# Products of constants on TensorE in the pauses of stage passages

## The chip, the cores and the metric

The program runs on one core of one Trainium2 chip. A core has TensorE (PE), VectorE (DVE), ScalarE (ACT) and GpSimd (POOL), with SyncE (SP) as a queue for transfers. The metric is the device time of one execution in microseconds, the median of several runs. Everything is float32; wide products use three fp32r products (high times high, high times low, low times high) in place of one fp32 product.

## The reference

Two model blocks run one after the other on 512 tokens of width 1024. The first has dilated attention beside a gated recurrence (HGRN2) and a mixture of experts, the second two layers with adaptive modulation: layer 0 with latent attention and a gated linear recurrence over 512 latent and 256 context tokens, layer 1 with a gated delta recurrence. Cut to what matters here:

```python
def first_block(x, ...):
    h = rmsnorm(x, norm1_g)
    proj = h @ w_in                                   # 1024 x 3584
    o_attn = dilated_attention(...); o_h = hgrn2(...)
    x = x + concat(rmsnorm(o_attn), rmsnorm(o_h) * silu(gh)) @ w_out
    x = x + hier_moe(rmsnorm(x, norm2_g), ...)
    return rmsnorm(x, norm_f_g)

def second_block(x, ...):
    for layer in range(2):
        a_lat = modulate(rms_norm(h_lat, norm1_w[layer]), ...)
        o_lat, o_ctx = even_mixer(...) if layer % 2 == 0 else odd_mixer(...)
        h_lat = h_lat + ml[2] * o_lat
        h_lat = h_lat + ml[5] * sq_relu_mlp(modulate(rms_norm(h_lat, norm2_w[layer]), ...), w1, w2)
        # layer 0 does the same to the 256 context tokens
    return rms_norm(h_lat, final_norm)
```

Every `rms_norm` needs a sum over the 1024 features before any value of the normed tile is known, and the product that follows needs the normed tile.

## The kernel before

Activations lie feature-major: `E.hT` is the residual, `E.aT` the work tile, each 128 partitions x 8 feature tiles x up to 768 tokens. The program is a row of stages. Each is one `nc.Block()` that gives every engine its own instruction list, and it ends in a barrier of all engines: the next stage starts when the last of them is through. Inside a stage the order on each engine is the order in which the code is written, and semaphores join the engines. At four places (after the experts, after latent attention, after the delta recurrence and after the second MLP) a cleanup of semaphores lies behind the barrier.

Stages that the change touches, with their lines:

- `gemm` (L436) is every large projection. Its PE list takes one unit after another (a PSUM bank of 128 features x 512 or 256 tokens, 24 matmuls of L531), eight k-steps of three products. It waits for `w_low` (the weight panel's low part, L596 on ACT and L599 on DVE) and, in the first unit or units, for `x_low` at each k-step: that is the tile's low part, made just then on DVE. With `split` (the three output projections `wout1`, `wout2`, `wout3`) ACT copies a high part (L579) and DVE subtracts (L582). With `normed` (`proj1`, `proj2`, `proj3`) the tile comes from a `Normed` object.
- `Normed` (L258) finishes a norm: `sums` on PE (L271, L272) adds the last squares over partitions, `root` on ACT (L277 to L281) takes the root, `lows` on DVE (L294, L303) scales and splits. `NormedOpening` has nothing for PE to do; `NormedTwice` folds two norms into one (L353 on PE, L358 to L370 on ACT, L379 to L415 on DVE).
- With `squares`, a gemm's evacuations also make the next norm's squares: ACT L246, POOL L254.
- `mlp` (L2069 on) begins with `normed.sums`, then L2128 takes its first weight slot k by k as `x_low` arrives, and L2143 the rest.
- `hgrn` ends with group sums (L1296), ACT's root, DVE's scale (L1406), POOL's gate (L1430). `mla_units` ends with output products (L2337) and ACT's copy (L2372). `short_conv` begins with the split of its weights (ACT L3188, DVE L3241), then L3143. `delta` ends with transposes (L3588) and eight scalings on DVE (L3790). `put_out` turns and stores the result (L3887, L3888, L3897).

A float32 matmul shows as two records in the trace, an fp32r matmul as one.

Of the kernel before, what the change touches and what calls it, by code (L numbers as in the profile page):

```python
# [99 lines left out]
def setup(nc, ctx, d):  # L100
# [18 lines left out]
    E.cst = lambda name: d["cst"][:, CST_AT[name][0]:CST_AT[name][0] + CST_AT[name][1]]  # L119
    return E  # L120


# [135 lines left out]
class Normed:  # L258

    def __init__(self, E, c, name, T, scale, shift):  # L260
        sb = lambda n: c.enter_context(E.nc.sbuf_tensor(f"{name}_{n}", [P, KT, T], mybir.dt.float32r))
        self.E, self.T, self.scale, self.shift = E, T, scale, shift
        self.segs = [(0, S)] + ([(S, T)] if T > S else [])
        self.high, self.low = sb("x_high"), sb("x_low")
        self.summed, self.rooted, self.scaled, self.x_high, self.x_low = (E.sem(f"{name}_{x}") for x in (
            "summed", "rooted", "scaled", "x_high", "x_low"))
# [41 lines left out]
class NormedOpening(Normed):  # L308

    def sums(self, pe):  # L310
        pass
# [22 lines left out]

class NormedTwice(Normed):


# [98 lines left out]
def gemm(E, name, jobs, banks=8, split=None, ahead=None, normed=None, squares=None, then_fetch=None, then=None, stream=None):  # L436
# [29 lines left out]
    with ExitStack() as c:  # L466
# [56 lines left out]
        def _(pe):  # L523
            before, panel = -1, -1
            if normed:
                normed.sums(pe)

            def parts_of(u, k):
# [15 lines left out]
            for u, (j, (mms, _, _, part)) in enumerate(units):  # L544
# [28 lines left out]
                if stream:  # L573
                    stream.beside(pe, u)

        def part_of_x(eng, me):
# [610 lines left out]
def hgrn(E, qkv, H, stream, project):  # L1187
# [11 lines left out]
    with ExitStack() as c:  # L1199
# [9 lines left out]
        with nc.Block() as block:  # L1209
# [12 lines left out]
            def _(pe):  # L1222
# [102 lines left out]
                stream.fold(pe, 1)  # L1325
                sums(3)

            @block.scalar
# [740 lines left out]
def mlp(E, layer, T, W, end, ring, next_weights):  # L2069
# [15 lines left out]
    with ExitStack() as c:  # L2085
# [12 lines left out]
        with nc.Block() as block:  # L2098
# [14 lines left out]
            def _(pe):  # L2113
                normed.sums(pe)
                with pe.Fori(0, CHUNKS) as chunk:
                    for st in range(2 * ST):
# [16 lines left out]
                        for u, (n, s, a, b) in enumerate(unit):  # L2133
# [5 lines left out]
                            for k in range(KT):  # L2139
                                if u == 0 and i == 0:  # L2140
                                    pe.wait_ge(h_low, NT + HT * chunk + k + 1)
                                for p, (w, x) in enumerate(((wh, high), (wh, low), (wl, high))):
                                    last = pe.matmul(bank(st, n, s, b - a), w[:, st % 2, k, n * P:(n + 1) * P], x[:, k, a:b],  # L2143
                                                     start=(k == 0 and p == 0), stop=(k == KT - 1 and p == 2))
                            last.then_inc(full, 1)

            @block.scalar
# [136 lines left out]
def mla_units(E, qh, kh, V, project):  # L2284
# [9 lines left out]
    with ExitStack() as c:  # L2294
# [6 lines left out]
        with nc.Block() as block:  # L2301
# [5 lines left out]
            def _(pe):  # L2307
# [33 lines left out]
                for t in range(n + 5):  # L2341
                    if t < n:
                        scores(t)
                    if 3 <= t <= n + 2:
                        turns(t - 3)
                    if t >= 5 and t % 2:
                        outputs((t - 5) // 2)

            @block.scalar
# [750 lines left out]
def short_conv(E, w, q, k, vc, xh, xl, ring, own, gates, constants):  # L3100
# [12 lines left out]
    with ExitStack() as c:  # L3113
# [7 lines left out]
        with nc.Block() as block:  # L3121
# [9 lines left out]
            def _(pe):  # L3131
                def turn_keys(m, bank):
                    for i, (ch, j) in enumerate((ch, j) for ch in (m, m + 1) for j in range(2)):
                        last = pe.transpose(E.bank(bank)[:, i * P:(i + 1) * P], k[:, ch, j].rearrange("a g t -> a (g t)"), E.ident)
                    last.then_inc(turned, 1)
                for n in range(tiles):
                    pe.wait_ge(w_low, n + 1)
# [156 lines left out]
def delta(E, G, O, room, more, gate_dram, project, constants):  # L3294
# [8 lines left out]
    with ExitStack() as c:  # L3303
# [25 lines left out]
        def region(u, r):  # L3329
# [13 lines left out]
            "W", "W_out", "KG", "ke", "qd", "N0"))  # L3343
        uu, ws, vna, vnv, ds, st, sg, oo, oadd, gate_in, os_, squared, rooted, normed_p, normed_v, turned = (sem(f"delta_{n}") for n in (
            "U", "WS", "vn_act", "vn_dve", "DS", "S", "SG", "O", "O_add", "gate_in", "OS", "squared", "rooted", "normed_pool",
            "normed_dve", "turned"))

# [21 lines left out]
        with nc.Block() as block:  # L3369
# [9 lines left out]
            def _(pe):  # L3379
# [197 lines left out]
                for late in range(2):  # L3577
                    for u, (i, h) in enumerate(out_units):
# [11 lines left out]
                        if late:  # L3590
                            last.then_inc(turned, 1)

            @block.scalar
# [83 lines left out]
            def _(dve):  # L3677
# [110 lines left out]
                for u, (i, h) in enumerate(out_units):  # L3788
                    dve.wait_ge(turned, u + 1)
                    dve.scalar_tensor_tensor(out=E.aT[:, i:i + 5:4, 256 * h:256 * h + 256], in0=E.bank(u).rearrange("p (g n) -> p g n", g=2),  # L3790
                                             scalar=E.v("gdn_o_norm_2", 0), in1=gate[:, i:i + 5:4, 256 * h:256 * h + 256],
                                             op0=ALU.mult, op1=ALU.mult)

# [161 lines left out]
```

## Time and profile before

| | us |
|---|---|
| median of 3 runs (2991.27 to 2994.41) | 2993.59 |
| span of the profiled execution | 2994.6 |
| PE busy in it | 2787.2 (93%) |
| VectorE, ScalarE, GpSimd busy | 1152.1, 940.6, 403.4 |

No time of its own is given for the profiled execution beyond its span; the span lies 1.0 us above the median, so sums made on the span are carried over to the median unchanged. A busy PE is not PE at its peak: the trace also has the granted clock of TensorE, 1.00 for the full 2.4 GHz and 0.50 for 1.2 GHz, for each stretch. Where PE has been still, or has done little, that clock is found at 0.50 some microseconds on. "Idle before" in a row is what the engine waited, with the instruction that ended it.

### The profile page before, as it was taken

What the parts mean: (1) busy time and instruction counts of PE and PEld (TensorE: products, weight loads), DVE (VectorE), ACT (ScalarE), POOL (GpSimd) and SP (SyncE); (2) the same over time, 40 slices, a digit from 0 to 9 for tenths busy, and PEclk for the clock granted to TensorE, in tenths of its full rate; (3) what the DMA queues carried; (4) which work ended last, traced back from release to release, by engine and by line L of the source; (5) the groups of instructions that cost most, each with busy time, mean ns of one, the idle gap of its engine ahead of it and who ended that gap; (6) DMA issues with size and microseconds to landing.
All of it is one profiled execution on the core that took longest, in us unless ns stands there. A gap on an engine that the chain in (4) does not pass through costs nothing. (4 is left out here: it accounts for less than half of the span.)

```text
span 2994.6 us, 50282 instructions
## 1 busy us (share of the span) xinstructions
PE 2787.2 (93%) x21610; PEld 2080.0 (69%) x21610; DVE 1152.1 (38%) x1626; ACT 940.6 (31%) x1542; POOL 403.4 (13%) x332
## 2 busy tenths in 40 slices
PE   8988889999998998999999999998997788799999
PEld 6764654444444884747878888887786777678887
DVE  3225342223324317264442323234344455443333
ACT  4235331111112226145331212123373445432222
POOL 0014120000001302045100000010002555200001
PEclk9999889999999999789999999999997899999999
DMA  6547719999994111000121212120310000223331
GB/s 243 197 149 271 264 57 386 402 403 406 400 404 155 49 43 57 24 29 1 57 71 57 70 56 70 56 70 28 103 49 30 4 4 4 87 97 98 98 97 57
DMA packets 153632, 389.56 MB, mean 130 GB/s; under 512 B 9471, under 2 KB 100506, under 8 KB 140666
## 3 DMA queue, kind: packets, MB, share of 16 engines
q1 hardware_dynamic: 141226, 198.40, 19.4%
q10 hardware_dynamic: 12240, 188.75, 15.4%
q8 instruction: 129, 2.11, 0.3%
q14 instruction: 37, 0.30, 0.0%
HBM read 381.36 MB, written 5.77 MB: 129 GB/s over the span
## 5 line engine op out<-in xcount | busy, mean ns | idle before, releaser
L2143 PE MATMUL ps<-mlp_h_low,mlp_w_high 128*128 128x512 f32 (+1 forms) x768 | 272.0, 354 | 0.0
L2143 PE MATMUL ps<-mlp_h_high,mlp_w_high 128*128 128x512 f32 (+1 forms) x768 | 271.9, 354 | 0.0
L2143 PE MATMUL ps<-mlp_h_high,mlp_w_low 128*128 128x512 f32 (+1 forms) x768 | 271.6, 354 | 0.0
L1997 ACT ACTIVATE mlp_w_high<-mlp_ring 128x2048 fp32r<-128x2048 f32 x64 | 122.2, 1912 | 316.2 <-PE ps L2143 316.2
L2143 PE MATMUL ps<-mlp_x_low,mlp_w_high 128*128 128x512 f32 (+1 forms) x576 | 204.0, 354 | 0.0
L2143 PE MATMUL ps<-mlp_x_high,mlp_w_high 128*128 128x512 f32 (+1 forms) x576 | 203.9, 354 | 0.0
L2143 PE MATMUL ps<-mlp_x_high,mlp_w_low 128*128 128x512 f32 (+1 forms) x576 | 203.7, 354 | 0.0
L254 POOL TENSOR_TENSOR aT<-aT 128x512 f32<-128x512 f32 (+1 forms) x30 | 59.6, 1986 | 1030.5 <-ACT aT L246 1029.9
L2001 DVE TENSOR_TENSOR mlp_w_low<-mlp_ring,mlp_w_high 128x2048 fp32r<-128x2048 f32 x64 | 146.5, 2292 | 62.8 <-ACT mlp_w_high L1997 62.8
L2207 DVE SCALAR_TENSOR_TENSOR hT<-ps,mod,hT 128x512 f32<-128x512 f32 x96 | 63.5, 661 | 256.0 <-PE ps L2143 256.0
L2143 PEld LDWEIGHTS ps<-mlp_h_high,mlp_w_high 128*128 128x128 f32 x768 | 145.2, 189 | 20.5
L2143 PEld LDWEIGHTS ps<-mlp_h_high,mlp_w_low 128*128 128x128 f32 x768 | 145.1, 189 | 20.2
L2143 PEld LDWEIGHTS ps<-mlp_h_low,mlp_w_high 128*128 128x128 f32 x768 | 145.3, 189 | 19.9
L1863 DVE TENSOR_TENSOR hT<-hT,ps 128x512 f32<-128x512 f32 x128 | 79.3, 682 | 181.4 <-PE ps L1699 181.4
L2196 DVE TENSOR_TENSOR mlp_square<-mlp_relu 128x768 f32<-128x768 f32 (+1 forms) x64 | 52.7, 825 | 249.1 <-ACT mlp_relu L2165 248.8
L2165 ACT ACTIVATE mlp_relu<-ps 128x512 f32<-128x512 f32 x96 | 49.7, 527 | 296.1 <-PE ps L2143 218.4
L3143 PE MATMUL ps<-odd_x_high,conv_w_parts 128*128 128x512 f32 (+1 forms) x448 | 121.3, 359 | 3.1 <-DVE conv_w_parts L3241 3.1
L2143 PEld LDWEIGHTS ps<-mlp_x_high,mlp_w_high 128*128 128x128 f32 x576 | 108.9, 189 | 15.4
L2143 PEld LDWEIGHTS ps<-mlp_x_low,mlp_w_high 128*128 128x128 f32 x576 | 108.9, 189 | 15.0
L2143 PEld LDWEIGHTS ps<-mlp_x_high,mlp_w_low 128*128 128x128 f32 x576 | 108.8, 189 | 15.1
L1704 PE MATMUL ps<-e_wu,aT 128*64 128x512 f32 x512 | 116.9, 598 | 0.0
L1704 PE MATMUL ps<-e_wg,aT 128*64 128x512 f32 x512 | 116.2, 595 | 0.7 <-ACT aT L1784 0.7
(561 smaller groups left out, 6011.0 us busy)
## 6 DMA issues: line engine op xcount, KB each, us to landing
mlp_ring<-in_mlp_w_dram SPq DMA_DIRECT2D x64, 1024.0 KB, 5.3
e_wg<-in_w_gate_dram ACTq DMA_DIRECT2D x15, 4096.0 KB, 14.7
e_wu<-in_w_up_dram ACTq DMA_DIRECT2D x15, 4096.0 KB, 14.3
ring<-in_w_down_dram ACTq DMA_DIRECT2D x15, 4096.0 KB, 13.8
ring<-in_ada_w_dram SPq DMA_DIRECT2D x16, 2048.0 KB, 8.9
h_rest<-in_ada_w_dram SPq DMA_DIRECT2D x8, 2048.0 KB, 8.5
ring<-in_w_in_dram SPq DMA_DIRECT2D x6, 2048.0 KB, 11.2
proj_ring<-in_even_w_in_dram SPq DMA_DIRECT2D x8, 1024.0 KB, 5.1
```

The costliest lines, as they stand in the source:

```text
L254: pool.tensor_tensor(total, self.square_of(self.E, 0, self.T) if n == 1 else total, self.square_of(self.E, n, self.T), ALU.add)\
L1704: last = pe.matmul(E.ps[SLOTS * s:SLOTS * (s + 1), bank * BANK:(bank + 1) * BANK], xg[:, par, k, half * P + s * SLOTS:half * P + (s + 1) * ...
L1863: dve.tensor_tensor(E.hT[:, n, 0:S], E.hT[:, n, 0:S], E.bank(4 + n % 4), ALU.add).then_inc(added, 1)
L1997: act.activation(self.high[:, slot], self.ring[:, slot], ACT.Copy).then_inc(self.w_high, 1)
L2001: dve.tensor_tensor(self.low[:, slot], self.ring[:, slot], self.high[:, slot].bitcast(FP), ALU.subtract).then_inc(self.w_low, 1)
L2143: last = pe.matmul(bank(st, n, s, b - a), w[:, st % 2, k, n * P:(n + 1) * P], x[:, k, a:b], start=(k == 0 and p == 0), stop=(k == KT - 1 a ...
L2165: act.activation(r[:, n, a:b], bank(st, n, s, b - a), ACT.Relu).then_inc(relus, 1)
L2196: dve.tensor_tensor(sq[:, n, :], r[:, n, :], r[:, n, :], ALU.mult).then_inc(squares, 1)
L2207: dve.scalar_tensor_tensor(out=E.hT[:, k, a:b], in0=bank(st, n, s, b - a), scalar=E.mod[:, layer, 40 + k, s:s + 1], in1=E.hT[:, k, a:b], o ...
L3143: last = pe.matmul(E.bank(2 * (n % 3) + half, b - a), wp[:, part, n % 2, kk, :], xp[:, kk, a:b], start=(kk == 0 and i == 0), stop=(kk == K ...
```

## The change

A helper issues a number of matmuls of two constant tiles (all ones as weights, the identity as data, both float32, 128 x 128) into a PSUM bank that nobody reads before it is written again. It is called at seventeen places: behind the norm's sums (20 in `proj1`, 32 in `proj2`, 18 in `proj3` and in each MLP), at the start of the three output projections (11), of the short convolution (12), and at the ends of stages (14 in `hgrn`, 6 in latent attention, 6 at the end of each output projection, 11 at the end of each MLP, 22 in `delta`). That is 233 matmuls. Where the bank may still be read, PE first waits: at an output projection's end for the evacuation of that bank, at an MLP's end for all evacuations but the last step's, in `delta` for the first of DVE's eight scalings, which gets a new semaphore. Nothing is taken out, and no other engine gets an instruction.

```diff
+def constant_products(E, pe, bank, count):
+    for _ in range(count):
+        pe.matmul(E.bank(bank, P), E.ones, E.ident, start=True, stop=True)
...
 class Normed:
+    pause = 18
 class NormedOpening(Normed):
+    pause = 20
 class NormedTwice(Normed):
+    pause = 32
...
@@ gemm, tensor
             if normed:
                 normed.sums(pe)
+                constant_products(E, pe, 0, normed.pause)
+            elif split:
+                constant_products(E, pe, 0, 11)
...
                 if stream:
                     stream.beside(pe, u)
+            if squares:
+                who, n = freed_at[len(units) - banks]
+                pe.wait_ge(freed[who], n)
+                constant_products(E, pe, len(units) % banks, 6)
@@ hgrn, tensor
                 stream.fold(pe, 1)
                 sums(3)
+                constant_products(E, pe, 5, 14)
@@ mlp, tensor
                 normed.sums(pe)
+                constant_products(E, pe, 0, normed.pause)
                 with pe.Fori(0, CHUNKS) as chunk:
...
                             last.then_inc(full, 1)
+                pe.wait_ge(added, U * (ST * CHUNKS + ST - 1))
+                constant_products(E, pe, 0, 11)
@@ mla_units, tensor
                         outputs((t - 5) // 2)
+                constant_products(E, pe, 0, 6)
@@ short_conv, tensor
+                constant_products(E, pe, 0, 12)
                 for n in range(tiles):
@@ delta, tensor
                             last.then_inc(turned, 1)
+                pe.wait_ge(first_out, 1)
+                constant_products(E, pe, 0, 22)
@@ delta, vector
+                    if u == 0:
+                        ins.then_inc(first_out, 1)
```

PE at the end of `delta` and the start of `wout3` before (L3588 are the transposes of the output, L3369 and L522 the ends and starts of blocks):

```order
L3380 MATMUL ps<-gdn_vn,gdn_qk 64x128 x16
L3588 MATMUL ps<-base,gdn_O 128x2x64 x32
L3369 UNCONDITIONAL_BRANCH
L522 UNCONDITIONAL_BRANCH
L531 MATMUL ps<-wout_x_high,wout_w_high 128x512
L531 MATMUL ps<-wout_x_low,wout_w_high 128x512
L531 MATMUL ps<-wout_x_high,wout_w_low 128x512
```

And with the change, where the helper is L126 and all lines lie some 12 to 25 further down:

```order
L3405 MATMUL ps<-gdn_vn,gdn_qk 64x128 x16
L3613 MATMUL ps<-base,gdn_O 128x2x64 x32
L126 MATMUL ps<-base 128x128 x22
L3394 UNCONDITIONAL_BRANCH
L534 UNCONDITIONAL_BRANCH
L126 MATMUL ps<-base 128x128 x11
L546 MATMUL ps<-wout_x_high,wout_w_high 128x512
L546 MATMUL ps<-wout_x_low,wout_w_high 128x512
```

Behind the last transpose stand 22 products ahead of the block's end, and 11 more stand ahead of the first real product of the next block.

PE at the end of `wout3` and the start of the second MLP before (L271 and L272 are the norm's sums; the two ISA rows set up the loop over the MLP's chunks):

```order
L531 MATMUL ps<-wout_x_low,wout_w_high 128x512
L531 MATMUL ps<-wout_x_high,wout_w_low 128x512
L466 UNCONDITIONAL_BRANCH
L2112 UNCONDITIONAL_BRANCH
L271 MATMUL ps<-aT,base 128x512
L272 MATMUL ps<-aT,base 128x512
```

And with the change:

```order
L126 MATMUL ps<-base 128x128 x6
L478 UNCONDITIONAL_BRANCH
L2132 UNCONDITIONAL_BRANCH
L279 MATMUL ps<-aT,base 128x512
L280 MATMUL ps<-aT,base 128x512
L126 MATMUL ps<-base 128x128 x18
L2136 UNCONDITIONAL_BRANCH
```

Six products follow the projection's last one, and 18 lie between the norm's sums and the loop whose first product waits for the normed tile.

## Rows read from the trace of the kernel before

**Rows 1.** The page: span of the profiled execution, and its instructions.

```profile
span 2994.6 us, 50282 instructions
```

**Rows 2.** Windows: stretch, us, busy us (xcount) PE/PEld/DVE/ACT/POOL, PEclk, DMA share, GB/s

```profile
23.05:28.63 5.58, 5.58 (x13) 4.42 (x14) 5.58 (x10) 2.53 (x4) 0.00 (x0) 0.50 1.05 410
345.60:349.50 3.90, 3.90 (x9) 3.11 (x10) 3.90 (x7) 3.11 (x6) 0.00 (x0) 0.50 0.80 244
967.27:970.70 3.43, 3.42 (x10) 2.85 (x11) 3.43 (x7) 1.48 (x3) 1.77 (x1) 0.50 0.00 0
1429.38:1434.90 5.52, 5.52 (x13) 4.41 (x14) 5.52 (x7) 4.54 (x6) 0.00 (x0) 0.50 0.69 268
1508.60:1513.40 4.80, 4.80 (x14) 4.06 (x15) 4.80 (x10) 2.24 (x4) 0.00 (x0) 0.50 0.01 2
2049.40:2052.70 3.30, 3.30 (x7) 1.52 (x5) 2.36 (x2) 2.23 (x2) 0.00 (x0) 0.50 0.00 0
2058.03:2063.00 4.97, 4.96 (x12) 3.95 (x13) 4.97 (x10) 2.24 (x4) 0.00 (x0) 0.50 0.00 2
2117.71:2121.00 3.29, 3.29 (x8) 2.61 (x9) 1.09 (x1) 0.00 (x0) 0.00 (x0) 0.50 1.08 398
2570.25:2575.00 4.75, 4.75 (x11) 3.77 (x12) 4.75 (x8) 3.11 (x6) 0.00 (x0) 0.50 1.01 353
2623.74:2629.60 5.86, 5.86 (x14) 4.60 (x15) 5.86 (x10) 2.90 (x5) 0.00 (x0) 0.50 0.35 121
```

**Rows 3.** Windows view: the pause ahead of the first projection, same columns.

```profile
16.40:18.40 2.00, 0.00 (x0) 0.00 (x0) 0.00 (x0) 1.73 (x4) 0.51 (x1) 1.00 1.07 405
18.40:23.05 4.65, 0.00 (x0) 0.03 (x1) 4.51 (x6) 2.28 (x4) 0.00 (x0) 0.50 1.05 409
```

**Rows 4.** Windows view of line 3897 at half and full clock, line 531 at full.

```profile
2981.50:2984.50 3.00, 3.00 (x14) 3.00 (x15) 0.50 0.00 0
2984.70:2989.70 5.00, 5.00 (x47) 5.00 (x46) 1.00 0.51 208
...
352.00:382.00 30.00, 30.00 (x135) 24.82 (x133) 1.00 0.50 216
```

**Rows 5.** Waits view of PE: us in total, times, longest us.

```profile
PE ps L2128 <- DVE mlp_x_low L303: 8.9, 2, 5.2
...
PE ps L531 <- DVE odd_x_low L303: 6.4, 4, 5.2
```

**Rows 6.** Timeline: how VectorE hands parts over, and where proj2's first units end.

```profile
977.04 1.84 DVE L415 SCALAR_TENSOR_TENSOR even_x_low<-aT,mod,even_x_high 128x512 fp32r<-128x512 f32 x2 [0.51 <-POOL even_x_high L427]
...
985.84 0.39 PE L531 MATMUL ps<-even_x_high,proj_w_high 128*128 128x512 f32 x1
...
1428.29 7.03 DVE L582 TENSOR_TENSOR wout_x_low<-aT,wout_x_high 128x768 fp32r<-128x768 f32 x8
```

**Rows 7.** Timeline: what ends last in four stages, and PE's last sums in hgrn.

```profile
336.76 2.05 PE L1296 MATMUL ps<-hg_sq,base 128*128 128x512 f32 x2
...
340.97 1.26 POOL L1430 TENSOR_TENSOR aT<-aT,h_rest 128x512 f32<-128x512 f32 x1 [3.98 <-DVE aT L1406]
...
1424.36 0.38 ACT L2372 ACTIVATE aT<-ps 128x256 f32<-128x256 f32 x1 [0.76 <-PE ps L2337]
...
2560.45 5.36 DVE L3790 SCALAR_TENSOR_TENSOR aT<-ps,vcol,gdn_vt 128x512 f32<-128x512 f32 x8 [1.39 <-PE ps L3588]
...
2975.67 1.26 POOL L254 TENSOR_TENSOR aT<-aT 128x512 f32<-128x512 f32 x1 [8.15 <-ACT aT L246]
```

**Rows 8.** Timeline of ACT ahead of proj3: the root's first step waits for PE.

```profile
2052.91 0.81 ACT L279 ACTIVATE aT<-ps 128x768 f32<-128x768 f32 x1 [1.26 <-PE ps L272]
```

**Rows 9.** Timeline: start of the short convolution (ACT, PE) and of the output stage.

```profile
2115.35 2.00 ACT L3188 ACTIVATE conv_w_parts<-odd_room 128x1024 fp32r<-128x1024 f32 x2 [8.41 <-PEq L466]
...
2117.71 0.80 PE L3143 MATMUL ps<-odd_x_high,conv_w_parts 128*128 128x512 f32 x1 [3.11 <-DVE conv_w_parts L3241]
...
2978.06 0.56 PE L3887 MATMUL ps<-base,aT 128*128 128x1 f32 x2 [3.13 <-PEq L3869]
```

## What the change should do to the time

> **What bounds the kernel now.** I read the page first, then the windows view over every 25 us, then the waits of PE, then the timeline around each place that the change touches. The profiled execution spans 2994.6 us [rows 1]; the median is 2993.59, and I take the sum from the median, since nothing hints that the 1.0 us between them would change. PE is busy 93% of it, so a microsecond taken off PE's own work counts unless something else is late there. The reader is to see in [rows 2] ten stretches in which PE works without a break and yet at a granted clock of 0.50, the 1.2 GHz level. Each lies behind a pause in which PE waited for a norm or for the high and low parts of a tile. [rows 3] shows how it comes about at the first projection: for two microseconds of stillness the clock is still 1.00, then it is 0.50, and it stays there until some microseconds of dense matmuls have gone by. The change fills such pauses with matmuls that nobody needs. So three questions set the time: do they hold the clock up, what is half-clock work worth where it stands, and where do they stick out of the pause.
>
> **What one product costs.** The trace has no product of ones and identity. The nearest is L3897: float32, 128 x 128, other weights each time, two records per matmul. At full clock some 46 records lie in 5.00 us, 0.11 each, so 0.22 us a product; at half clock 14 lie in 3.00 us, so 0.43 [rows 4]. I take 0.22 where PE was at work until shortly before. The same rows say that this form counts as work for the clock: it ran at 0.50, and behind it the clock was 1.00. Calls of 6, 11, 12, 14, 18, 20, 22 and 32 are then 1.3, 2.4, 2.6, 3.1, 4.0, 4.4, 4.8 and 7.0 us.
>
> **What the full clock is worth, stage by stage.** A 512-wide fp32r product takes 5.58/13 = 0.43 us at half clock [rows 2], and at full clock 30.00 us hold 135 records with those cut by the edges, so about 0.225 [rows 4].
> - `proj1`: 13 products in 5.58 us would take 2.93, a gain of 2.6. VectorE's parts come no slower than PE takes them, and PE does not wait again behind the first.
> - `wout1`: 9 products, 3.90 against 2.03, gain 1.9. `wout3`: 11, 4.75 against 2.48, gain 2.3. MLP of layer 1: 14, 5.86 against 3.15, gain 2.7.
> - `wout2` has 768 tokens, and VectorE's eight parts take 7.03 us, to 1435.32 [rows 6], 0.88 each against 3 x 0.225 = 0.68 of PE. With full clock the first unit ends at 1435.32 + 0.68 = 1436.0. Before, 13 of 24 were done at 1434.90 [rows 2], and 11 more end at 1437.4. Gain 1.4, not the 2.8 that half of 5.52 would be.
> - `proj2`: the part that came late ends at 977.04 + 1.84 = 978.88 [rows 6], and three k-steps lie behind it. One is six 512-wide and six 256-wide products, 1.35 + 0.7 = 2.05 to 2.1 us. So the first units end at 985.0 to 985.2 in place of 985.84 [rows 6]. Gain 0.6 of the 1.7 that half of 3.43 would be.
> - MLP of layer 0: half of 4.80 is 2.4; its k-step costs VectorE about as much as PE, so I take 2.2.
> - `proj3`: of PE's four waits for `odd_x_low` only one is 5.2 us, and three share 1.2 [rows 5]. These three come later: PE had caught up with VectorE although it began at half clock. Gain 0.1.
>
> That is 2.6 + 1.9 + 2.3 + 2.7 + 1.4 + 0.6 + 2.2 + 0.1 = 13.8 us.
>
> Two more come from elsewhere. Eleven products at the end of layer 0's MLP lie beside the last evacuation, square and addition there, and keep the clock up for the sums ahead of `proj3`, which ran at 0.50 [rows 2]. ACT waited 1.26 us for them [rows 8], behind its table load: gain 1.3, and if the clock falls in between, 0. In `short_conv` the first tile's stretch of 3.29 us at half clock [rows 2] would give 1.6.
>
> **Where the products stick out.** A stage ends when its last engine is through.
> - `hgrn`: PE's sums end at 338.81 less the drain, POOL's gate at 342.23 [rows 7]. Fourteen take 3.1 us if the clock is up, 6.0 if not. It is at 0.50 there, but PE has then been at work for three microseconds and the clock should rise within a few of the products. Cost between 0 and 0.9 (all of them slow: 2.6); I take 0.3.
> - Latent attention: PE is through at about 1424.3, ACT at 1424.74 [rows 7]. Six more end at 1425.6: cost 0.9, since behind this barrier everything starts, ACT's split of the next tile too. It would be 2.2 at half clock.
> - `delta`: the first of the eight scalings ends at 2561.1, the last at 2565.81 [rows 7]; 22 products end at 2566.0 to 2566.3 with the drain: cost 0.4, at half clock up to 2.5.
> - Layer 1's MLP: PE had been idle for 3.13 us when it began L3887 at 2978.06 [rows 9], that is from 2974.93. Eleven end at 2977.3, POOL's addition ended at 2976.93 [rows 7]: cost 0.4. In return the output stage starts at full clock. Its first sixteen records are one column wide and may not hold it. I take 1.1 for the stage with the 0.4 taken off; the bounds are -0.4 (clock falls at once) and +3 (it holds all through 6.5 us that ran at half).
> - Short convolution: the block starts at 2115.35, its first real product at 2117.71 [rows 9]. Twelve end at 2118.0: cost 0.3.
> - Layer 1's MLP start: the shorter wait for `mlp_x_low` is 8.9 - 5.2 = 3.7 us [rows 5], 18 products are 4.0. Cost 0.2.
> - The other calls are covered: 20 in `proj1` by the 6.65 us of [rows 3], 32 in `proj2` and 18 in two places by DVE's scaling and ACT's root, which nothing of PE holds up; 11 ahead of each output projection by ACT's copy and DVE's two subtractions; 6 at an output projection's end by the last evacuation and ACT's square. If that cover were gone, each would cost its own 1.3 to 7.0.
>
> The added wait in `delta` queues nothing behind it but the products. DVE, ACT, POOL and the queues get no work, and their loads start as PE frees them.
>
> **The sum.** 13.8 + 1.3 + 1.6 + 1.1 - 0.3 - 0.9 - 0.4 - 0.3 - 0.2 = 15.7 us, so 2993.6 - 15.7 = 2977.9, say 2978.
>
> **Rivals.**
> 1. *Every half-clock microsecond gives back half.* The gated stretches are worth more than I grant because VectorE's lead is not as thin as I read it. The eight tile stretches of [rows 2] last 38.8 us together, half is 19.4 against my 13.8: 15.7 + 5.6 = 21.3, so 2972. Against it speak the waits of [rows 5] and the pace of L582. The Trainium skill, "TensorE: Matmul & The Clock Gate", terms table, gives the penalty of throttled time as that time times one less the clock's share, which is this 19.4; the trace agrees on the price of one product and not on what the stage gets.
> 2. *The tails are slow.* In `hgrn`, latent attention and `delta` the work ahead is thin, and the clock is down when the products begin: 2.3 + 1.3 + 2.1 more, and `wout2` starts behind it with its eleven products late, 1 more: net 9, so 2985.
> 3. *The loads become late.* In `proj1` and `wout3` the DMA share is 1.05 and 1.01 [rows 2]; if the weights there come no earlier than before, those 2.6 and 2.3 go, and `short_conv` (1.08) with 1.3: 2984. Against it: PE has no wait for a load in these stages, and each panel is split a unit ahead.
> 4. *Slower: constants do not count as work.* Then the clock falls as before, and each call costs 0.43 a product. 20 (8.6 us) stick out of their pause by 2.9, 32 (13.8) by 5, 11 ahead of output projections (4.7) by 1.6 three times, 18 (7.7) by 2.5 to 4 three times, 12 by 2.8, 22 by 4.7, 14 by 2.6, the tails of 6 and 11 by some 5: together about 36, so 3030. It decides as soon as the calls run at half clock throughout; with a rise in each it is rival 2. L3897 speaks against it.
> 5. *Nothing much.* The clock falls once more between the last product and the real work, where gaps of 0.7 to 2 us stay. Two thirds of the gain go: 2989.
>
> **How the numbers follow.** My forecast has 0.56, rival 1 0.12, rival 2 0.12, rival 3 0.08, rival 4 0.04, rival 5 0.08. A measurement of this kernel can tell about 0.2%, 6 us, from no change. Faster by more: the forecast and rivals 1 to 3, 0.88, less 0.02 for the edges: 0.86. Within: 0.10. Slower: 0.04. The range takes in rivals 1 to 3 and the unknown of the tails: 2970 to 2987.
>
> **What would show it.** In the profile after, the ten stretches should show a clock near 1.00 at the first real products, the products 0.22 us each, `proj3` and `proj2` end their first units hardly sooner, and the barrier behind latent attention and `delta` should open later by 0.9 and 0.4. I am wrong if the products show 0.43 in most places, or if the first units end no earlier although the clock is up.

## The result

The changed kernel takes 2965.93 us (median of 6 runs, 2958.55 to 2969.06) against 2990.02 us (6 runs, 2977.62 to 2994.41) of the kernel before; the ratio is 0.9922, with a 95% interval of 0.9904 to 0.994. Forecast were 2978 us, between 2970 and 2987. The direction was right, the time lies 12 us under the forecast and 4 under the end of the range. The gain read off the ratio is 23 us, between 18 and 29; 15.7 had been forecast. Of the six executions of before three are those that the forecast's 2993.59 rests on; the other three, timed later, have a median of 2984.62.

The page of the profiled execution (2956.7 us, where before had 2994.6, [rows 1]) and the row with the span and the mean granted clock:

```profile
span 2956.7 us, 51214 instructions
...
PE 2801.8 (95%) x22076; PEld 2104.2 (71%) x22076; DVE 1151.6 (39%) x1626; ACT 940.7 (32%) x1542; POOL 404.5 (14%) x332
```

```profile
core 0: 2956.7 us, clock 0.977
```

The same row of before:

```profile
core 0: 2994.6 us, clock 0.956
```

The 233 products made PE busier (2801.8 us, 2787.2 before) and the kernel shorter. Next, windows of PE of the changed kernel (stretch, us, PE busy (records), granted clock, DMA share, GB/s): the call in `proj1`, the first real products behind ten of the calls, and at last the output stage.

```profile
17.60:22.31 4.71, 4.70 (x40) 1.00 1.06 412
23.23:26.25 3.02, 3.02 (x13) 1.00 1.05 405
341.90:343.95 2.05, 2.05 (x9) 1.00 0.80 177
958.40:962.50 4.10, 4.10 (x26) 1.00 0.00 0
1414.40:1417.40 3.00, 3.00 (x11) 1.00 1.05 410
1492.23:1495.10 2.87, 2.87 (x16) 1.00 0.03 10
2029.90:2032.60 2.70, 2.70 (x9) 1.00 0.00 0
2038.30:2041.30 3.00, 2.60 (x10) 1.00 0.03 8
2098.40:2101.60 3.20, 3.20 (x16) 1.00 0.92 328
2538.40:2540.90 2.50, 2.50 (x11) 1.00 1.06 367
2589.90:2593.10 3.20, 3.20 (x15) 1.00 0.51 182
2941.60:2947.00 5.40, 5.40 (x34) 0.69 0.01 3
```

These answer [rows 2]: every stretch that ran at 0.50 there is at 1.00 here, and thirteen records of `proj1` lie in 3.02 us in place of 5.58. The first row gives the price of a product: 40 records in 4.70 us, 0.235 us a product, where 0.22 was assumed. Of these places only the output stage still has a part at the lower clock.

PE's waits (us in total, times, longest) where it now meets VectorE:

```profile
PE ps L546 <- DVE odd_x_low L311: 4.3, 7, 1.6
...
PE ps L546 <- DVE wout_x_low L601: 1.3, 3, 0.6
PE ps L2149 <- DVE mlp_x_low L311: 1.2, 1, 1.2
```

In `proj3` four waits have become seven ([rows 5]): PE is faster and waits for VectorE more often, and the first units end no sooner (61.34 us in both, in the table below). That is what the forecast put at 0.1 us.

### The profile page after: what moved, and what is told of

Read it like the earlier page. It is cut to its first block and busy times, and to the rows that moved or that the text cites. A ratio compares the mean times of both kernels' runs of the same rounds, so it can differ in the third digit from the quotient of the medians.

```text
span 2956.7 us, 51214 instructions
## 1 busy us (share of the span) xinstructions
PE 2801.8 (95%) x22076; PEld 2104.2 (71%) x22076; DVE 1151.6 (39%) x1626; ACT 940.7 (32%) x1542; POOL 404.5 (14%) x332
## 3 DMA queue, kind: packets, MB, share of 16 engines
q10 hardware_dynamic: 12240, 188.75, 15.7%
```

## Where the time went between the two traces

The two spans differ by 37.9 us, more than the medians do. I followed pairs of operations of VectorE, ScalarE and GpSimd, which are the same in both kernels, through both traces, and took the time from one to the next. 16 us of the difference lie at the calls, 22 in stages that no call touches; most of these are light stages, with short matmuls and waits between the engines. The two largest are the delta recurrence (8.3 us, taken up at the end) and the middle of latent attention with its gated recurrence (7.8 us). The windows of the second in the changed kernel, and in a second execution of the very same program (run `e5_changed_again`, below), same columns:

```profile
1197.90:1295.70 97.80, 92.26 (x454) 0.83 0.05 18
```

```profile
1201.80:1307.50 105.70, 99.16 (x462) 0.74 0.05 17
```

One program, the same instructions, 97.8 and 105.7 us, with a clock of 0.83 and 0.74. Before took 105.6, as long as the second execution of the changed kernel, so 7.8 of the 22 us can't be put down to the change: single executions differ by that much. The Trainium skill, "TensorE: Matmul & The Clock Gate", Part 1, says that the number of matmuls at the lower clock varies between runs of one kernel; the two rows agree. It also puts the penalty of the ramp at under 1% of a typical kernel's span. Here the clock's row of before, 0.956, is well above that, and the mere spread of before's executions is 24 us, 0.8%.

The Trainium skill's terms table in "TensorE: Matmul & The Clock Gate" prices throttled time at that time times one less the clock's share. The profile's mean clock already has that share in it, so by its two rows the price is 2994.6 x 0.044 less 2956.7 x 0.023, or 64 us; the spans differ by 38. As a rule for the difference of these two traces it is an upper bound; for one stage where PE waits for other engines in part of the time, run `e10_rope_too` below shows why.

## Experiments

`e1`, `e8`, `e9` and `e13` are the kernel before with the products that are named and no other; all others are the changed kernel with calls taken out, or moved where said. Each was timed in 6 to 12 executions (`e9` in one), beside 23 to 28 of before on the same chip. The ratio has its 95% interval behind it; a difference "by the medians" is the plain one. The two can make the size of an effect differ by up to 5 us, and both are given where it matters.

**The size of the effect, and a repetition.** No edit.

```diff
 (the changed kernel as it is)
```

> The changed kernel again, against more executions of before: before was 2983.6 us by the median of 28 executions in the last call, 10 us under its first three. If my sum of 15.7 us is right and the first executions of before were slow ones by chance, the ratio is 0.9947 and lies below 0.9965 and above 0.993. If the 22 us beyond the sum that the two traces show belong to the change, it is 0.9922 or less.

Measured: 2966.05 us (6 runs), ratio 0.9918 (0.989 to 0.9945). All executions of before beside the experiments of this section, 101 of them, have a median of 2985.5 us between 2974.6 and 2998.7, and 20 of them lie at or over 2991.2. The three on which the forecast's level stood were all over 2991.2. Twelve executions of the changed kernel have 2966.05. So 8 of the 12 us by which the forecast's time was off are the level, and the effect is 19.5 us by these medians. By the two ratios (0.9922 and 0.9918) it is 23 to 24. The expectation had named a ratio of 0.9947, between 0.993 and 0.9965, if 15.7 us were right, and that did not come: even the upper end of the interval, 0.9945, is below it, and the ratio itself is at the value (0.9922 or less) that stood for a gain beyond the sum. The effect is therefore larger than the forecast's, by 4 us as the medians have it and by 8 as the ratios have it.

**`proj1` alone.**

```diff
+    pause = 20   (NormedOpening; no other call, every other pause 0)
```

> The kernel before with the 20 products of proj1 and none of the other calls. The whole change gained 24 us by its median, and its trace shows 16 of them where the prediction put them and 22 us in stages that no call touches. Theory A (the rest is a matter of where the light stages come to lie in time: any shift ahead of them moves them into or out of half clock): proj1 gains 2.5 us, and the trace shows latent attention, its recurrence and delta some us shorter or longer than in the trace of before although not one of their instructions is another; the ratio is 0.9992 with up to 0.003 either way. Theory B (products at the ends of stages hold the clock up into the light work behind them): nothing but proj1 changes beyond some tenths of a us, ratio 0.9992. Theory C (luck of single executions, the same in both kernels): ratio 0.9992, and the trace differs from before's in the light stages, but the median does not.

Measured: 0.9983 (0.9968 to 0.9997), 2981.33 against 2983.57 us by the medians, 2.2 us. All three theories had 0.9992, which the interval holds, so the time decides between none of them. The trace has the first unit at 12.65 us between two evacuations around it, against 15.26 in before. The middle of latent attention took as long as in before (105.6), delta 290.2 in place of 294.0, with nothing of them edited.

**A mere delay.** Three products in the middle of `proj2`, where PE is at work at full clock without a break.

```diff
+                if isinstance(normed, NormedTwice) and u == 12:
+                    constant_products(E, pe, u % banks, 3)
```

> The kernel before with three products in the middle of proj2, where PE is at work at full clock without a break, and nothing else: a pure delay of 0.7 us of all that follows. In four of the six traces the middle of latent attention, with the gated recurrence, took 105.6 us with 54.6 at half clock, in two 97.9 with 34.1, and the two began 1 us later against the steps of the clock. Theory A (when the light stages begin decides how much of them runs at half clock): the stretch takes 97.9 us although it only starts 0.7 later, and the kernel as a whole is 2 to 7 us faster than before, by a mere delay. Rival (what the change's products do for the clock decides): the stretch takes 105.6 as before, and the kernel is 0.7 us slower.

Measured: 0.9998 (0.9984 to 1.0011). The window of the same middle of latent attention:

```profile
1207.20:1301.10 93.90, 88.68 (x466) 0.85 0.06 19
```

11.7 us shorter than in before, behind a delay alone, though the part ahead of it took 4.5 more (101.6 against 97.1). Theory A had expected a shorter stage and a kernel faster by 2 to 7 us; the second did not come. That the delay is what made the stage shorter is not shown: it is one trace, and the changed kernel gave 97.8 and 105.7 us without any edit. In sixteen traces this middle took 105.6 to 105.8 us seven times and 93.1 to 99.0 nine times, with and without the change's calls. So the stage falls into one of a few lengths in each execution, and neither the calls nor the delay is shown to choose it.

**The ends of stages, without and alone.** Taken away (`e2`), alone (`e3`), and alone with the 18 products in the MLPs (`e7`).

```diff
 e2_no_ends (each with its wait, where it has one)
-                constant_products(E, pe, 5, 14)               (hgrn)
-                constant_products(E, pe, len(units) % banks, 6)   (output projections)
-                constant_products(E, pe, 0, 11)       (end of mlp)
-                constant_products(E, pe, 0, 6)        (mla_units)
-                constant_products(E, pe, 0, 22)       (delta)
```

> The changed kernel without the products at the ends of stages (14 in hgrn, 6 in latent attention, 6 at output projections, 11 in the MLPs, 22 in delta); those behind norms' sums and at starts of output projections and of the short convolution stay. By the terms of the sum: the tails cost 0.3, 0.9 and 0.4 less, and what they brought goes: 1.3 ahead of proj3 and 1.1 in the output stage, so within 1 us of the changed kernel, some 15 to 24 us below before, ratio about 0.994. Theory B (ends hold the clock for light work behind): the 8 us beyond my sum go, ratio 0.996 or above, and the routing behind wout1 runs at half clock as in before. Theory A: as the terms say, with up to 6 us either way from the light stages.

Measured: 0.9953 (0.9935 to 0.997), 12.4 us under before by the medians: some 7 less than the changed kernel, where at most 1 had been expected. Its trace gives about half of that. The sums ahead of `proj3` take their 1.2 us again and the output stage 1.2 more than in the changed kernel, and 1.1 comes back behind latent attention. And without the tails the eleven ahead of `wout1` and `wout3` run at a clock of 0.57 and 0.53 (4.55 and 4.89 us in place of 2.69) and stick out, which makes each of these stages some 1 us longer. The forecast had no term for this tie between a tail and the call behind it.

```diff
 e3_ends_alone
-    pause = 20, 32, 18                            (the three classes)
+    pause = 0
-                constant_products(E, pe, 0, 11)       (output projections)
-                constant_products(E, pe, 0, 12)       (short_conv)
```

> The kernel before with the products at the ends of stages alone (14, 6, 6, 6, 6, 11, 11, 22). By the terms of the sum: gain 1.3 ahead of proj3 and 1.1 in the output stage, cost 0.3, 0.9, 0.4, and the output projections behind hgrn, latent attention and delta start with the clock up if it outlives the pause of 2 us behind them: 0.8 to 6 us faster, ratio 0.998 to 1.000. Theory B: 8 us or more, ratio 0.997 or below. Theory A: as the terms say, with up to 6 us either way.

Measured: 1.0011 (0.9995 to 1.0028), 5.0 us slower by the medians, which alone is within the noise; by the terms it was to be 0.8 to 6 us faster. Its trace has what those of before, the changed kernel, `e1`, `e2` and `e4` have not. First PE's waits in layer 0's MLP in this kernel:

```profile
PE ps L2147 <- issue: 6.6, 3, 2.4
```

Three pauses without a releaser, each where the loop over the MLP's chunks starts again. The transfer queue that brings instructions (packets, MB, share), in the MLP of the kernel before, and then in this one:

```profile
q8 instruction: 5, 0.08, 0.1%
```

```profile
q8 instruction: 33, 0.54, 0.4%
```

The same queue in the three turns behind the first alone, in this kernel; in before and in the changed kernel it has no packet at all there:

```profile
q8 instruction: 26, 0.43, 0.4%
```

So the loop's code is brought in anew in every turn, and PE stands for 1.8 to 2.4 us at its head; the stretch takes 529.4 in place of 520.5 us. The call at the end of `hgrn` and those at other ends have put 32 more products into PE's code ahead of this loop.

```diff
 e7_ends_and_mlp = e3_ends_alone, and
+                constant_products(E, pe, 0, normed.pause)   (mlp; pause had been set to 0)
```

> The run with the ends alone, plus the 18 products behind the sums in both MLPs. The run before showed three pauses of 1.8 to 2.4 us of PE in layer 0's MLP, each where its loop starts again, that nothing released; before and the changed kernel have none. Theory D (the place of the loop in PE's code decides, and the 32 products ahead of it moved it): with 36 more instructions ahead of the loop it lies elsewhere, the three pauses change or go, and the kernel gains up to 8.9 us beyond the 2.1 + 2.7 of the two MLP starts: 13 us below the run with the ends alone. Theory E (something else in that execution, such as a late transfer): the MLPs gain 4.8, and medians of the two runs differ by 5.

This run did not test its question: with `pause` at 0 the added call issues nothing, and the program is `e3` once more. As a repetition it shows that the pauses belong to the program: 529.9 us with three pauses again, ratio 1.0008 (0.9991 to 1.0026).

**Where the loop lies in PE's code.** `e9` puts 32 products into the middle of `proj2` and has none of the change's calls; it was timed once.

```diff
+                if isinstance(normed, NormedTwice) and u == 12:
+                    constant_products(E, pe, u % banks, 32)
```

> The kernel before with 32 products in the middle of proj2, where PE is at work at full clock. No call of the change is in it; ahead of the MLP's loop stand 32 products more, as many as in the run with the ends alone. Theory D (where PE's loop lies in its code decides): the three pauses of about 2 us that nothing releases are there again where layer 0's MLP starts its loop anew, the MLP's stretch takes 529 us in place of 520.5. Rival (the pauses come from the products at the ends themselves): 520.5. The stretch proj2 is 7.5 us longer either way.

PE's waits in its MLP, and one of the pauses in the timeline (start, us, engine, line, operation, idle time before it and what ended that):

```profile
PE ps L2144 <- issue: 7.0, 3, 2.5
```

```profile
1635.12 0.47 PE L2144 MATMUL ps<-mlp_x_high,mlp_w_high 128*128 128x512 f32 x1 [2.16 <-issue]
```

The stretch takes 529.8 us, and 33 instruction packets; the one execution took 2991.48 us. With as many products ahead of the loop, all of them some 500 us before it and none at the end of a stage, the pauses are back. So the products at the ends are not their cause as such; what the two programs share is how far down PE's code the loop lies. `e11` takes the 14 of `hgrn` out of `e3`, which leaves 18 ahead of the loop.

```diff
 e11_ends_no_hgrn = e3_ends_alone, and
-                constant_products(E, pe, 5, 14)
```

> The run with the ends alone, without the 14 of hgrn, so 18 products ahead of the MLP's loop in place of 32. Theory D: no pauses at the loop, 520.5 us there, and the kernel 9 us below the run with all ends: ratio 0.998, of which 1.3 ahead of proj3 and 1.1 in the output stage. Theory E: still 529 and a ratio of 1.001.

Measured: 0.9978 (0.9961 to 0.9995), 2979.89 us, 8.7 under the median of `e3`, as theory D had it; 5 packets, 520.5 us, no pause. `e12` is the changed kernel less 20 products, 104 ahead of the loop.

```diff
 e12_no_mla_hgrn
-                constant_products(E, pe, 5, 14)
-                constant_products(E, pe, 0, 6)        (mla_units)
```

> The changed kernel without the six behind latent attention and the 14 of hgrn. By the sum hgrn's call costs 0.3 and gives nothing: 0.3 less than without latent attention's alone. Rival: without the 14 the eleven ahead of wout1 run at half clock, as behind delta in the runs without its 22, and wout1 starts later: 1 to 2 us more.

Measured: 1.0023 (1.0006 to 1.0041), slower than before by the interval though by little, 25 to 27 us above `e6` and `e5` by the medians; no more than 2 had been expected. The expectation's rival held, but it is small beside that: without the 14 the eleven ahead of `wout1` ran at 0.56 and `wout1` ended 1.4 us later behind its barrier. Its trace, windows over 20 us around a start of the loop in this kernel, and then in the changed one:

```profile
1620.00:1640.00 20.00, 14.86 (x81) 0.91 0.18 55
```

```profile
1620.00:1640.00 20.00, 20.00 (x119) 1.00 0.17 52
```

And PE's waits in this MLP:

```profile
PE ps L2148 <- DVE mlp_w_low L2020: 15.0, 3, 5.2
```

Three pauses of 4.7 to 5.2 us, behind each of which the clock is at 0.50 for some microseconds; the stretch takes 542.5 us in place of 520.5, with 33 packets. The pauses are 15.0 us of the 22, the rest is work at the lower clock. The profile puts them down to the weights' low part; but in the changed kernel PE goes on at the loop's head at 1625.91 us while VectorE's split of that step starts at 1628.06, so it can't be what is waited for. Pauses came with 32 and 104 products ahead of the loop, none with 0, 3, 18, 20, 92, 118, 124 and 136. I have no rule for the place. (92 lies between 32 and 104 and has none, so it is no simple limit. A repeat every 64 products would fit all ten counts, since 32 and 104 are then 32 and 40 and the others lie at 0 to 28 and 54 to 60; that is a guess from two counts with pauses, and nothing tests it.) Why they last 2 us in one kernel and 5 in the other is open as well.

**The tails behind latent attention and delta.**

```diff
 e6_no_mla
-                constant_products(E, pe, 0, 6)        (mla_units)
 e4_no_mla_delta: that, and
-                pe.wait_ge(first_out, 1)
-                constant_products(E, pe, 0, 22)
```

> The changed kernel without the six products behind latent attention. Terms of the sum: 0.9 to 1.1 us less than the changed kernel, since wout2 started with the clock up in the run without them too. Rival: with them gone the pause behind latent attention lets the clock fall in part of the executions, 1.4 us more: +0.4.

> The changed kernel without the 6 products behind latent attention and the 22 behind delta (with their wait). The terms give 0.9 + 0.4 = 1.3 us less than the changed kernel if the eleven at the start of wout2 and wout3 are enough to hold or raise the clock, ratio to before about 0.992. Rival: without the tails the clock falls before the eleven are through and the first real products run at half clock for up to 3.4 us: 1.4 and 2.3 are lost again, net 2.4 us slower than the changed kernel.

Measured: 0.9932 (0.991 to 0.9954) and 0.9945 (0.9923 to 0.9967); neither can be told from the changed kernel by the whole time. By the traces the time from a point in latent attention to the last operation of `wout2` is 190.17 us with the six in three traces, and 189.08 without them in four: they cost 1.1, and 0.9 was forecast. In a fifth trace without them, of `e10` below, the eleven at the start of `wout2` ran at the lower clock, and the stage ended 0.85 later:

```profile
1415.67:1420.71 5.04, 5.04 (x23) 0.50 0.76 266
```

Without the 22 of delta the eleven ahead of `wout3` run at half clock (the window of `e4`) and stick out:

```profile
2538.34:2543.06 4.72, 4.72 (x23) 0.55 0.75 229
```

The stretch of delta's end and `wout3` then takes 49.0 to 49.2 us, 48.2 with the 22 at full clock, 49.7 without any call. But the 22 are not sure of their clock: in seven of the nine traces that have them they took 5.18 us and opened the barrier 0.6 later, in the other two (`e11`, `e12`) they ran at 0.75, took 6.8 us and opened it 2.2 later. In `e12` nothing of the gain in `wout3` was left.

**Products in the pauses of another stage.** Behind the gated recurrence PE waited three times for VectorE (1.5 to 1.9 us) and then ran at half clock.

```diff
 e10_rope_too = e6_no_mla, and in swap(i)
+                        if i in (2, 3, 4):
+                            pe.wait_ge(logged, 4)
+                            constant_products(E, pe, 0, 6)
```

> The changed kernel without the six behind latent attention, and with six products each ahead of the third, fourth and fifth rope product, where PE waited 1.5 to 1.9 us for VectorE and then ran 17 us at half clock (in traces of before and of the changed kernel). If the pauses are what takes the clock, those 17 us run at 1.00 and the stretch up to the keys gets 4 to 6 us shorter, ratio 0.991 or less. Rival (the narrow products of the stage themselves let the clock fall: 32 x 512 and 64-row outputs): the stretch stays, and three calls that stick out cost 0 to 1.5 us.

Measured: 0.9946 (0.9925 to 0.9966), no gain on `e6`. The stretch from the first to the last of these products in `e6`, and in `e10`:

```profile
1273.57:1306.50 32.93, 27.86 (x52) 0.74 0.00 0
```

```profile
1266.41:1298.26 31.85, 28.10 (x88) 0.89 0.00 1
```

The expectation was 4 to 6 us if the pauses are what takes the clock. It rose from 0.74 to 0.89, and only 1.1 us came of it. PE's own work fell by some 4.6 us (28.10 less three calls of 1.60, against 27.86), and the calls put 4.8 back. In seven traces without these products the stretch took 29.5 to 29.9 us, in seven 32.9 and in one 33.6: chance between executions is worth more here than the products.

**The short convolution.** The traces put 4 to 5 us of the gain into the delta recurrence, which has no call but its last.

```diff
 e13_conv_alone: all calls at 0 but
+                constant_products(E, pe, 0, 12)       (short_conv)
 e14_no_conv: the changed kernel less this call
-                constant_products(E, pe, 0, 12)       (short_conv)
```

> The kernel before with the 12 products at the start of the short convolution and no other call. Theory F (this call also makes the turning stage and the delta recurrence shorter): 2.9 in the convolution, 1.3 in the turning stage and about 4 in delta, so 8 us faster, ratio 0.9973. Rival G (chance of the traces): 2.9 in the convolution alone, ratio 0.999, delta at 292 to 294 us.

> The changed kernel without the convolution's 12 products. Theory F: 8 us slower than the changed kernel, ratio to before 0.995, delta at about 293 us. Rival G: 2.9 slower, ratio 0.993, delta at 286 to 293.

Measured: 0.9971 (0.9952 to 0.9989) alone, and 0.9944 (0.9926 to 0.9962) without it. The windows of delta in the first and in the second:

```profile
2262.40:2556.80 294.40, 227.49 (x7544) 0.91 0.07 24
```

```profile
2250.40:2534.90 284.50, 224.69 (x7592) 0.95 0.08 26
```

With the call alone delta took as long as ever, and without it it was the shortest of all. Both speak against theory F, by which the convolution's call makes delta shorter; they are single traces of a stage that took 285.5 and 290.5 us in two executions of the changed kernel, so they don't exclude it. The convolution with the turning stage behind it took 152.6 us on average in eight traces with the call and 155.3 in eight without. The whole times speak the other way: `e13` was forecast at 0.9973 by theory F and 0.999 by rival G and came to 0.9971, with 0.999 just outside its interval; `e14`'s 0.9944 allows both (0.995 and 0.993). In microseconds the call is worth 3 to 6 by the medians and 7 to 9 by the ratios, against 2.6 in the traces. Between F and G the runs don't decide.

## Why the forecast was right and where not

The terms, each as the time between two operations around the place, averaged over the traces (five have no call near there: before, `e1`, `e8`, `e9`, `e13`; six have all or nearly all: the changed kernel, `e4`, `e5`, `e6`, `e10`, `e14`; where a term allows it, more). The differences are those of the unrounded means.

| term | forecast | measured |
|---|---|---|
| `proj1` | 2.6 | 2.2 (14.9 to 12.6) |
| `hgrn`'s end and `wout1` | 1.9 - 0.3 | 1.1 (71.0 to 69.8) |
| `proj2` | 0.6 | 0.4 (32.1 to 31.75) |
| latent attention's end and `wout2` | 1.4 - 0.9 | 0.05 (190.22 to 190.17) |
| layer 0's MLP, first units | 2.2 | 1.95 (26.98 to 25.03) |
| sums ahead of `proj3` | 1.3 | 1.25 (5.71 to 4.46, which `e9` also had once) |
| `proj3` | 0.1 | 0.0 (61.34, both) |
| short convolution, turning stage | 1.6 - 0.3 | 2.6 (155.3 to 152.6) |
| delta's end and `wout3` | 2.3 - 0.4 | 1.5 (49.7 to 48.2) |
| layer 1's MLP, first units | 2.7 - 0.2 | 2.6 (22.0 to 19.4) |
| output stage, with the MLP's end | 1.1 | 1.4 (14.2 to 12.8) |
| sum | 15.7 | 15.0 |

**The terms were right in kind, and their sum in part by luck.** The sum is 15.0 against 15.7, and no single term is off by more than 1.3. But the eight tile stretches with their tails gave 9.8 in place of 12.0, and the convolution, the sums and the output stage 5.2 in place of 3.7; the two errors nearly cancel. The means also hide a spread: `hgrn`'s end came 0 to 1.2 us later, and the output stage gained nothing in one of the six traces (`e10`) and 2.7 us in three. The two doubts that mattered came out as forecast: constants count as work for the clock, and PE's gain is lost where VectorE is just as slow (`proj2`, `wout2`, `proj3`). Rival 4 is refuted; so are rival 3 (no stage waits for its weights more than before) and rival 5. Rival 1, half of every half-clock microsecond, gave 19.4 for the eight tile stretches; the traces give 9.8 with the tails' cost in it. Its time of 2972 was nearest to the measured one, and by luck alone: nothing of its mechanism is in the traces. Rival 2, slow tails, came true only in single executions: the barrier behind latent attention opened 1.1 us later (0.9 forecast), that behind delta 0.6 (0.4), and 2.2 in two traces of nine.

**Too small: the short convolution.** The forecast counted the first 3.29 us at half clock alone. Before has another such stretch some ten microseconds on, and the turning stage behind begins at half clock in five of eight traces without the call, and in one of eight with it. In the changed kernel the first two tiles' stretch is at 0.92; it was at 0.79 in before. Windows of before, then of the changed kernel:

```profile
2117.71:2141.60 23.89, 23.89 (x180) 0.79 0.30 101
```

```profile
2098.40:2118.70 20.30, 20.30 (x180) 0.92 0.30 106
```

**Too large: `wout2` and `wout3`.** The start of `wout2` gave 1.15 in place of 1.4 and its tail took it all. In `wout3` 22 and 11 products together gave 1.5 in place of 1.9.

**The step that failed first: the level.** "I take the sum from the median, since nothing hints that the 1.0 us between them would change." Three executions within some 3 us of each other looked like a firm number, and they were three of the longer ones of a spread of 24 us: 2993.59 against 2985.5, the median of 101. That is 8 of the 12 us. The profiled execution of before was longer still. Its span of 2994.6 us seemed to fit the median, but in all other runs the time of an execution is 1.8 us or more above its span, so this one took at least 2996.4 us, more than 95 of the 101. In it light stages stood at half clock for long: the rows of one trace are one draw of that. And the range of 2970 to 2987 was made of rivals and tails alone, with nothing in it for the level.

**The step that failed second: stages between the calls at nothing.** The sum has no term for any stage that has no call, and for delta only its last products. The effect is 19.5 us by the medians and 23 to 24 by the ratios, and the terms' places give 15.0. The 4.5 to 9 us that are left lie in what the sum put at nothing. Delta is 293.3 us on average in the five traces without calls (290.2 to 294.3) and 288.6 in the six with (284.4 to 293.6), 4.7 less, so that is where the traces show a part. The windows of all of delta in before and in the changed kernel show the clock that goes with it:

```profile
2271.90:2565.80 293.90, 226.46 (x7552) 0.92 0.07 25
```

```profile
2247.70:2533.30 285.60, 224.61 (x7593) 0.95 0.08 26
```

**What stays open.** Which call brings the 4.7, or whether one does, the runs do not settle; two executions of the changed kernel differ by as much. It goes with the calls behind the sums and at the starts rather than with the ends: `e2`, which has no ends, has 287.1, and the three traces with ends alone have 290.5, 292.8 and 293.5. But `e6`, which has all the starts, has 293.6. Of the convolution's call the two traces speak against it and the whole times for it. Runs with these calls taken out one by one, and delta read in several traces of each, would be needed.

**A rival that was missing.** A version that differs from the changed kernel by 20 products is slower than before. None of my rivals had it: products cost not only their time on PE, they also move the code behind them, and in three of the programs here that cost 9 or 22 us. That the changed kernel, with 124 products ahead of the loop, has no pause is luck.

## What to carry to other kernels

Filling a pause of TensorE with products of constants pays where the work behind it is dense and TensorE is what the stage waits for; the gain is then half of the stretch that ran at the lower clock, less what VectorE cannot follow (2.2 us of 2.8 in `proj1`, nothing in `proj3`), and it is nearly nothing in a stage of short steps between engines (1.1 us in `e10`). Whoever adds or removes instructions on TensorE ahead of a long loop should look, in the profile after, at the loop's head and at the packets of the instruction queue: that can cost more than the edit brings. And the level of a kernel with many short stages is known only from dozens of executions: take the sum from many of them, put their spread into the range, and compare ratios, not a new time with three old ones.

## What the runs showed of the hardware

Code that lies elsewhere can make a loop of matmuls fetch its instructions in every turn: 33 packets of instructions in place of 5 in four turns, and pauses of TensorE of 1.8 to 2.5 us in two programs and of 4.7 to 5.2 us in a third, three in each trace; the one program that was traced twice (`e3`, `e7`) shows them in both. A stage with unchanged instructions takes 93 to 106 us by how much of it falls to the lower clock, and 97.8 or 105.7 in one and the same program. And 22 products of constants behind thin work begin at either clock: they took 5.18 us in seven traces and 6.8 in two.
